# The first two units in thirds of the tokens, and a new order at the start of attention, in a one-core encoder kernel

## The chip, the cores and the metric

One core of one Trainium2 chip runs the whole network. Its engines work side by side and wait for each other on semaphores only: TensorE (PE; PEld is its weight load), VectorE (DVE), ScalarE (ACT), GpSimd (POOL) and SyncE (SP), which here only issues DMAs. The metric is the device time of one execution in microseconds (us), as the median of several runs. In an order of instructions "ps<-xh,wsp" reads: written tile, then read tiles.

## The reference

Two layers over 1040 tokens (16 meta tokens and 1024 real ones) of width 1024, all in f32. Only the beginning matters here:

```python
h = jnp.concatenate([meta, x], axis=1)
hn = rms_norm(h, mix_norm_gain[layer])
z = h @ w_in                                   # w_in: 1024 x 1536
u, q, k, v = jnp.split(z, [D_FOURIER, D_FOURIER + D_ATTN, D_FOURIER + D_ATTN + D_KV], axis=-1)
y_f = fourier_mix(u)                           # a 2-D DFT, real part
q = apply_rope(rms_norm(q...), cos, sin); k = apply_rope(rms_norm(k...), cos, sin)
y_a = attention(q, k, v)                       # 6 query heads, 2 key heads
return jnp.concatenate([y_f, y_a], axis=-1) @ w_out
```

After that come the MLP, a second mixer (hgrn2), a second MLP and a last norm.

## The kernel before

Tokens lie along the free axis, 1044 columns with 4 pads, in three thirds of CB = 348 columns; `h`, `xh` and `xl` are tiles of 8 rows k (the 1024 features over 128 partitions). A product with f32 accuracy is made from two roundings of each operand, a high and a low part: weights `raw` (512 KB, two slots) are split by POOL into `wsp` (L596 high, L598 low), activations by ACT (`xh`, L691) and DVE (`xl`, L1170). A *unit* is one product of all tokens with 128 columns of weights: for each k the three products high*high, high*low, low*high, each over the three thirds, so 72 matmuls of 348 or 344 columns into three banks of PSUM (`ps`), L1799.

**The start.** SP issues, in program order, the small rows, the meta tokens, the eight tiles of x (`xst`, L456), the weights of units 0 and 1 (`raw`, L463), two tables (`dftf`, `sint`), four pieces of the DFT table `tabs` (L481 with 105 partitions, L482 with 101 partitions, for c = 0 and 1), then the weights of unit 2 and on, each of which waits only until the slot has been split. PE turns the nine tiles (L1786, 64 transposes of 128 columns), DVE copies them to `h` (L1166), ACT squares them, then makes `xh` for each k over all tokens, DVE makes `xl`. Units 0 and 1 follow on PE; amid unit 1 stands `first_bcast` (L1845, L1849), which spreads the norm's factors into `rms`, and behind it ACT issues the load of `cost` on its own queue (L732). Then unit 2, the first step of the DFT (L1870), unit 3, the second step (L1888), and units 4 to 11.

POOL splits the weights of unit u when they have landed (`w_land`) and when unit u-1 has begun (`w_used`), so that their slot of `wsp` is free. PE begins unit u when `w_split` says that they are split.

**Attention.** 60 steps; step s scores a tile of 116 queries (L1942, nine matmuls into banks 0 to 2), DVE takes the maximum (three reductions, L1365, then L1367 and L1370), ACT makes the exponentials (L807) and the scaled copy (L819), and PE turns the probabilities (L1969). PE begins the scores of step s when the exponentials of s-1 are made; the transposes of step s-1 need banks 3 to 5, in which the first turned pieces of V lie until DVE has made their low halves `vtl` (L1306, five pieces `v_low(0)` to `v_low(4)`, in banks 3 to 7). `q_join(7)` (L1300) adds the two parts of the last query head, which no step needs before much later.

Of the kernel before, what the change touches and what calls it, by code (L numbers as in the profile page):

```python
# [17 lines left out]
F32 = mybir.dt.float32  # L18
F32R = mybir.dt.float32r
U8 = mybir.dt.uint8  # L20
ALU = mybir.AluOpType
# [3 lines left out]
P = 128  # L25
# [53 lines left out]
def encoder(nc, x, meta, mix_gain, ab_w_in, q_gain, k_gain, ab_w_out, c_w_in, lb_logits, o_gain,  # L79
# [3 lines left out]
    with ctx:  # L83
# [33 lines left out]
        xst = at("xst", [P, 9, 1024], F32, o_x)  # L117
# [114 lines left out]
        v_init = sem("dve_init")  # L232
        n_hi = sem("x_high")
# [126 lines left out]

        def pieces(a):
            return a.rearrange("p (a b) -> p a b", b=CB)
# [84 lines left out]
        def _(sp):  # L447
# [7 lines left out]
            for i in range(1, 9):  # L455
                nc.sync.dma_start(xst[:, i, :], x_rows[(i - 1) * P:i * P, :]).then_inc(s_x[i], 16)  # L456
# [18 lines left out]
            for j, col in enumerate(AB_COLS):  # L475
                load(U_MIX0 + j, j % 2, k8, v_in[:, :, col * P:(col + 1) * P], first=j < 2)
                if j == 1:
                    nc.sync.dma_start(dftf[:], dft_feat).then_inc(s_tab, 16)
                    nc.sync.dma_start(sint[:], sin_tab).then_inc(s_tab, 16)
                    for c in range(2):  # L480
                        nc.sync.dma_start(tabs[0:DN, c, 0:4, :], dft_tok[c, 0:4 * DN].rearrange("(j p) m -> p j m", p=DN)).then_inc(s_tab, 16)  # L481
                        nc.sync.dma_start(tabs[0:HALF + 1 - 4 * DN, c, 4, :], dft_tok[c, 4 * DN:HALF + 1]).then_inc(s_tab, 16)  # L482
# [193 lines left out]
        def _(act):  # L676
# [4 lines left out]
            for i in range(9):  # L681
# [6 lines left out]
            def first_high(k):  # L688
                act.wait_ge(t_dve, 18)
                act.wait_ge(x_sq, 9)  # L690
                A(xh[:, k, :], h[:, k, :], ACT.Copy, scale=small[:, NORM_COL[0] + k:NORM_COL[0] + k + 1]).then_inc(n_hi, 1)  # L691
# [36 lines left out]
            for k in range(KT):  # L728
                first_high(k)
# [414 lines left out]
        def _(dve):  # L1144
# [17 lines left out]
            for i in range(9):  # L1162
                t0, n = in_block(i)
                for half in range(2):
                    dve.wait_ge(t_rdy, 2 * i + half + 1)
                    V.tensor_copy(h[:, 4 * half:4 * half + 4, t0:t0 + n], ps[:, (2 * i + half) % 8, :].rearrange("p (k t) -> p k t", k=4)[:, :, 0:n]).then_inc(t_dve, 1)  # L1166

            def first_low(k):
                dve.wait_ge(n_hi, k + 1)
                V.scalar_tensor_tensor(xl[:, k, :], h[:, k, :], small[:, NORM_COL[0] + k:NORM_COL[0] + k + 1], xh[:, k, :],  # L1170
                                       ALU.mult, ALU.subtract).then_inc(n_lo, 1)
# [39 lines left out]
            dve.wait_ge(t_dve, 18)  # L1211
            clear_pads()
            for k in range(KT):
                first_low(k)
# [136 lines left out]
            def attend(b, s):  # L1351
# [35 lines left out]
            v_low(0)  # L1387
            v_low(1)
            q_scales()
            q_join(7)  # L1390
# [377 lines left out]
        def _(pe):  # L1768
# [6 lines left out]
            for i in range(9):  # L1775
                t0, n = in_block(i)
                pe.wait_ge(s_x[i], 16)
                for half in range(2):
                    g = 2 * i + half
                    if g == 7:  # L1780
                        pe.wait_ge(g_cp, 1)
                    if g >= 8:

                        pe.wait_ge(t_dve, g - 7)
                    for k in range(4):
                        ins = nc.tensor.transpose(ps[:, g % 8, k * P:k * P + n], xst[0:n, i, (4 * half + k) * P:(4 * half + k + 1) * P], ident[0:n, 0:n])  # L1786
                    ins.then_inc(t_rdy, 1)

            pe.wait_ge(t_dve, 18)
# [69 lines left out]
            unit(0, 0, 0, 0, hx, lx, x_ready(0))  # L1859
            unit(1, 1, 1, 1, hx, lx, gap=[first_bcast])  # L1860
# [69 lines left out]
            def attend(b, s):  # L1930
# [411 lines left out]
```

## Time and profile before

| | |
|---|---|
| median of 3 runs | 2677.04 us (2675.21 to 2677.28) |
| the profiled execution, its own time | 2674.69 us |
| its span on the page | 2672.9 us |
| PE busy | 2607.0 us, 98% |
| DVE, ACT, POOL busy | 58%, 34%, 42% |
| mean granted TensorE clock | 0.993 |

The span is what the profiler saw between the first and the last instruction; the execution's own time is 1.79 us more. All times inside the kernel are read from this one execution, counted from the start of the span.

### The profile page before, as it was taken

The page shows a single profiled execution, that of the slowest core. Times are in us where ns is not written, and L with a number is a line of the kernel's source. Part 1 is how long each engine was busy: PE and PEld are TensorE (multiplying, and loading weights), DVE is VectorE, ACT ScalarE, POOL GpSimd, SP SyncE. Part 2 cuts the span into 40 slices and gives each one's busy share as a digit, 9 for nine tenths or more (in the row PEclk, how much of TensorE's full clock was granted, in tenths as well). Part 3 has the DMA queues.
Part 4 walks back from the last instruction along what each step waited for, and adds up shares of the span by engine and source line. Part 5 has one row for each costly group of instructions (what it writes and reads, how often), then busy time and mean ns, then how long its engine had stood idle before and what let it go on. Part 6 is the DMA issues. An engine that isn't in the chain of part 4 may idle for free.

```text
span 2672.9 us, 44728 instructions
## 1 busy us (share of the span) xinstructions
PE 2607.0 (98%) x18627; PEld 2346.5 (88%) x18627; DVE 1553.9 (58%) x1843; ACT 913.3 (34%) x1496; POOL 1125.8 (42%) x599
## 2 busy tenths in 40 slices
PE   7998999999999999999999999999999999999998
PEld 7997998999999999999888888887877888788887
DVE  5398887465545433335676777778485444444444
ACT  3117886133333100013344344434243333210003
POOL 3240001347777444444232232234337878444441
PEclk9999999999999999999999999999999999999999
DMA  5110000122233322222111111112112333422221
GB/s 164 32 40 1 0 0 11 45 80 96 104 113 127 120 96 96 96 86 98 41 33 36 38 33 38 36 33 92 42 49 103 105 117 107 142 99 95 94 88 71
DMA packets 175990, 193.42 MB, mean 72 GB/s; under 512 B 7762, under 2 KB 145316, under 8 KB 175814
## 3 DMA queue, kind: packets, MB, share of 16 engines
q1 hardware_dynamic: 157238, 152.29, 17.4%
q10 hardware_dynamic: 18576, 38.55, 3.8%
q8 instruction: 138, 2.26, 0.4%
q14 instruction: 38, 0.31, 0.0%
HBM read 148.61 MB, written 42.21 MB: 71 GB/s over the span
## 4 chain that ended last, share of the span: by engine, by line
PE 83%; DVE 8%; issue 4%; ACT 3%; DMA 1%; POOL 1%; SPq 0%; ACTq 0%; DVEq 0%; POOLq 0%
PE ps L1799 53%; PE ps L2055 9%; PE ps L2052 5%; PE ps L2053 5%; PE ps L1942 3%; PE ps L2153 2%; PE ps L2121 1%; PE ps L2091 1%; DVE kk L1638 1%; DMA tmp<-hidden 1%; ACT prob L807 1%; PE ps L1888 1%; PE ps L2191 1%; ACT kk L1018 1%; DVE kk L1635 1%
## 5 line engine op out<-in xcount | busy, mean ns | idle before, releaser
L596 POOL TENSOR_TENSOR wsp<-raw,ones 128x1024 fp32r<-128x1024 f32 x140 | 275.2, 1966 | 1340.6 <-PE ps L1799 1303.5
L1799 PE MATMUL ps<-xh,wsp 128*128 128x348 f32 (+2 forms) x2624 | 622.8, 358 | 9.3 <-POOL wsp L598 6.1
L1799 PE MATMUL ps<-hh,wsp 128*128 128x348 f32 (+1 forms) x2480 | 546.2, 350 | 0.0
L1799 PEld LDWEIGHTS ps<-xh,wsp 128*128 128x128 f32 x2624 | 449.5, 189 | 54.9 <-issue 11.5
L1799 PEld LDWEIGHTS ps<-hh,wsp 128*128 128x128 f32 x2480 | 428.8, 188 | 44.1
L598 POOL TENSOR_TENSOR wsp<-raw,wsp 128x1024 fp32r<-128x1024 f32 x140 | 398.0, 2843 | 11.0
L1799 PE MATMUL ps<-xl,wsp 128*128 128x348 f32 (+2 forms) x1312 | 333.9, 351 | 0.0
L1799 PE MATMUL ps<-hl,wsp 128*128 128x348 f32 (+2 forms) x1240 | 313.9, 350 | 0.0
L1799 PEld LDWEIGHTS ps<-xl,wsp 128*128 128x128 f32 x1312 | 232.4, 189 | 24.3
L1799 PEld LDWEIGHTS ps<-hl,wsp 128*128 128x128 f32 x1240 | 218.1, 188 | 22.3
L910 ACT ACTIVATE hh<-tmp 128x1040 fp32r<-128x1040 f32 (+1 forms) x64 | 68.3, 1068 | 491.5 <-DMA tmp<-hidden 369.6
L1411 DVE TENSOR_TENSOR h<-h,ps 128x1024 f32<-128x1024 f32 x80 | 97.5, 1219 | 207.9 <-PE ps L1799 202.3
L1412 DVE TENSOR_TENSOR h<-h,ps 128x1044 f32<-128x1044 f32 x72 | 89.4, 1241 | 219.4 <-PE ps L1799 217.2
L618 POOL TENSOR_TENSOR wop<-sw,wop 128x512 fp32r<-128x512 f32 x112 | 144.3, 1298 | 69.3 <-ACT wop L876 69.2
L618 POOL TENSOR_TENSOR wop<-raw,wop 128x512 fp32r<-128x512 f32 x84 | 132.4, 1576 | 68.1 <-ACT wop L876 68.1
L1460 DVE SCALAR_TENSOR_TENSOR hid<-hid,rms 128x520 f32<-128x520 f32 (+1 forms) x112 | 150.9, 1365 | 0.9
L881 ACT ACTIVATE hid<-hid 128x520 f32<-128x520 f32 (+1 forms) x112 | 71.0, 634 | 229.3 <-DVE hid L1460 229.3
L1466 DVE TENSOR_TENSOR hl<-tmp,hh 128x1040 fp32r<-128x1040 f32 (+1 forms) x64 | 122.3, 1911 | 39.5 <-ACT hh L910 39.5
L1044 ACT ACTIVATE kp<-kk 128x512 f32<-128x512 f32 x112 | 65.6, 635 | 164.0 <-PE ps L2153 145.9
L2055 PE MATMUL ps<-xh,wop 128*128 128x512 f32 x336 | 109.5, 393 | 0.0
L876 ACT ACTIVATE wop<-sw 128x512 fp32r<-128x512 f32 x112 | 70.4, 629 | 113.4 <-PE ps L2053 48.2
L608 POOL TENSOR_TENSOR sw<-sw,raw 128x512 f32<-128x512 f32 x56 | 91.3, 1631 | 2.2
(311 smaller groups left out, 4971.1 us busy)
## 6 DMA issues: line engine op xcount, KB each, us to landing
raw<-in_w SPq DMA_DIRECT2D x128, 512.0 KB, 3.9
raw<-in_c_w_in SPq DMA_DIRECT2D x40, 512.0 KB, 3.8
tmp<-hidden SPq DMA_DIRECT2D x32, 520.0 KB, 4.2
tmp<-hidden SPq DMA_DIRECT2D x32, 512.0 KB, 4.2
hidden<-hid ACTq DMA_DIRECT2D x56, 260.0 KB, 2.1
hidden<-hid ACTq DMA_DIRECT2D x56, 256.0 KB, 2.1
raw<-in_ab_w_in SPq DMA_DIRECT2D x12, 512.0 KB, 3.7
xst<-in_x SPq DMA_DIRECT2D x8, 512.0 KB, 6.5
```

Source lines behind the costliest of these rows:

```text
L596: nc.gpsimd.tensor_tensor(wsp[:, slot, 0, :], raw[:, slot, :], one, ALU.mult).then_inc(w_high, 1)
L598: nc.gpsimd.tensor_tensor(wsp[:, slot, 1, :], raw[:, slot, :], wsp[:, slot, 0, :], ALU.subtract).then_inc(w_split, 1)
L608: nc.gpsimd.tensor_tensor(a[:], left, right, op).then_inc(t_add, 1)
L618: nc.gpsimd.tensor_tensor(operand(g, 1), a, operand(g, 0), ALU.subtract).then_inc(t_low, 1)
L1411: return V.tensor_tensor(real_pieces(h[:, k, :]), real_pieces(h[:, k, :]), real_outp(s), ALU.add).then_inc(z_free, 1)
L1412: return V.tensor_tensor(pieces(h[:, k, :]), pieces(h[:, k, :]), outp(s), ALU.add).then_inc(z_free, 1)
L1460: V.scalar_tensor_tensor(hid_[b][:], hid_[b][:], 0.0, rms[:, span(layer, b % 2)], ALU.max, ALU.mult).then_inc(t_relu, 1)
L1466: V.tensor_tensor(hl[t // CH % 2][:, t % CH, where], tmp[:, t % 2, where], hh[t // CH % 2][:, t % CH, where], ALU.subtract).then_inc(l_l, 1)
L1799: ins = M(ps[:, 3 * s + c, 0:n], w(a, k), b(k)[:, c0:c0 + n], start=(k == first and a == 0 and b is xa), stop=(k == last and a == 1))
L2052: M(out[:, 0, :], left, x(k)[:, 0:width // 2], start=start, stop=stop)
L2053: ins = M(out[:, 1, :], left, x(k)[:, width // 2:width], start=start, stop=stop)
L2055: ins = M(out, left, x(k), start=start, stop=stop)
```

## The change

1. **The order of loads.** The weights of unit 0 are issued ahead of the tiles of x, those of unit 1 behind the third tile. `tabs` comes next, then the weights of unit 2; `dftf` and `sint` stand behind these, with a wait for the last transpose and the last square, since `xst` now lies on their place (it no longer lies on `xh` and `xl`).
2. **Units 0 and 1 by thirds.** ACT and DVE make `xh` and `xl` in pieces of 348 columns, the first third as soon as tiles 0 to 3 are copied. PE makes third(0,0), third(1,0), third(0,1), third(1,1), third(0,2), `first_bcast`, third(1,2), 24 matmuls each (third(u,c): unit u, third c); the transposes of tiles 4 to 8 stand in between, in banks 6 and 7. `w_used` for unit 1 comes with the first matmul of third(1,2).
3. **The start of attention.** `v_low(0)` and `v_low(1)` move from ahead of step 0 to behind its reductions, `q_join(7)` and `v_low(2)` behind its reciprocal, `v_low(3)` and `v_low(4)` into step 1. PE waits for single pieces of `vtl` ahead of the transposes of steps 1 and 2.

```diff
-            for i in range(1, 9):
+            def x_load(i):
                 nc.sync.dma_start(xst[:, i, :], x_rows[(i - 1) * P:i * P, :]).then_inc(s_x[i], 16)
...
+            in_load(0)
+            for i in range(1, 4):
+                x_load(i)
+            in_load(1)
+            for i in range(4, 9):
+                x_load(i)
+            for c in range(2):
+                nc.sync.dma_start(tabs[0:DN, c, 0:4, :], ...).then_inc(s_tab, 16)
+                nc.sync.dma_start(tabs[0:HALF + 1 - 4 * DN, c, 4, :], ...).then_inc(s_tab, 16)
+            in_load(2)
+            sp.wait_ge(t_rdy, 18)
+            sp.wait_ge(x_sq, 9)
+            nc.sync.dma_start(dftf[:], dft_feat).then_inc(s_tab, 16)
+            nc.sync.dma_start(sint[:], sin_tab).then_inc(s_tab, 16)
+            for j in range(3, 12):
+                in_load(j)
...
-            for k in range(KT):
-                first_high(k)
+            for i in range(3):
+                x_square(i)
+            first_high(0)
+            for i in range(3, 6):
+                x_square(i)
+            first_high(1)
+            for i in range(6, 8):
+                x_square(i)
+            first_high(2)
+            x_square(8)
...
-            dve.wait_ge(t_dve, 18)
+            for i in range(4):
+                x_copy(i)
+            dve.wait_ge(t_dve, 8)
             clear_pads()
             for k in range(KT):
-                first_low(k)
+                first_low(0, k)
+                if k in (1, 3, 5):
+                    x_copy(4 + k // 2)
+            x_copy(7)
+            x_copy(8)
+            for c in range(1, 3):
+                for k in range(KT):
+                    first_low(c, k)
             first_norm()
...
                 if not begun(b, s, 1):
-                    dve.wait_ge(r_q, 6)
-                    for g in range(2, 5):
-                        v_low(g)
+                    v_low(0)
+                    v_low(1)
+                elif not begun(b, s, 2):
+                    v_low(3)
+                    v_low(4)
                 if not drained(b, s, 0):
                     dve.wait_ge(a_exp, b * 6 + (s + 1))
                     V.reciprocal(col[6], col[5]).then_inc(a_rc, 1)
+                if not begun(b, s, 1):
+                    q_join(7)
+                    dve.wait_ge(r_q, 6)
+                    v_low(2)
...
-            v_low(0)
-            v_low(1)
             q_scales()
-            q_join(7)
...
-            unit(0, 0, 0, 0, hx, lx, x_ready(0))
-            unit(1, 1, 1, 1, hx, lx, gap=[first_bcast])
+            def third(u, c, turns=()):
+                c0, n = ALL[c]
+                if c == 0:
+                    pe.wait_ge(w_split, u + 1)
+                for k in range(KT):
+                    if u == 0:
+                        pe.wait_ge(n_hi if c == 2 else f_hi, k + 1 if c == 2 else 8 * c + k + 1)
+                        pe.wait_ge(n_lo if c == 2 else f_lo, k + 1 if c == 2 else 8 * c + k + 1)
+                    for a, b in ((0, hx), (0, lx), (1, hx)):
+                        ins = M(ps[:, 3 * u + c, 0:n], wsp[:, u, a, k * P:(k + 1) * P], b(k)[:, c0:c0 + n],
+                                start=(k == 0 and a == 0 and b is hx), stop=(k == KT - 1 and a == 1))
+                        if u == 1 and c == 2 and k == 0 and a == 0 and b is hx:
+                            ins.then_inc(w_used, 1)
+                    if k % 2 and k // 2 < len(turns):
+                        x_turn(turns[k // 2])
+                if c == 2:
+                    ins.then_inc(z_ready, 1)
+
+            third(0, 0, (4, 5, 6))
+            third(1, 0, (7, 8))
+            third(0, 1)
+            third(1, 1)
+            third(0, 2)
+            first_bcast()
+            third(1, 2)
             unit(2, 0, 2, 0, hx, lx)
...
                     pe.wait_ge(a_p, b * 6 + s)
-                    if not begun(b, s, 2):
-                        pe.wait_ge(av_l, 5)
                     for r in range(3):
+                        if not begun(b, s, 3):
+                            pe.wait_ge(av_l, r + 1 if s == 1 else (4, 5, 5)[r])
```

SP's queue before, from the meta tokens to the weights of units 2 and on:

```order
L454 DMA xst<-in_meta 16x1024
L456 DMA xst<-in_x 128x1024 x8
L463 DMA raw<-in_ab_w_in 128x8x128 x2
L478 DMA dftf<-in_dft_feat 128x256
L479 DMA sint<-in_sin_tab 128x1044
L481 DMA tabs<-in_dft_tok 105x4x522
L482 DMA tabs<-in_dft_tok 101x522
L481 DMA tabs<-in_dft_tok 105x4x522
L482 DMA tabs<-in_dft_tok 101x522
L463 DMA raw<-in_ab_w_in 128x8x128 x10
```

And in the changed kernel, up to the weights of unit 3 and on:

```order
L460 DMA xst<-in_meta 16x1024
L470 DMA raw<-in_ab_w_in 128x8x128
L463 DMA xst<-in_x 128x1024 x3
L470 DMA raw<-in_ab_w_in 128x8x128
L463 DMA xst<-in_x 128x1024 x5
L493 DMA tabs<-in_dft_tok 105x4x522
L494 DMA tabs<-in_dft_tok 101x522
L493 DMA tabs<-in_dft_tok 105x4x522
L494 DMA tabs<-in_dft_tok 101x522
L470 DMA raw<-in_ab_w_in 128x8x128
L498 DMA dftf<-in_dft_feat 128x256
L499 DMA sint<-in_sin_tab 128x1044
```

The two small tables have left their place ahead of `tabs`; the four pieces of `tabs` still stand ahead of the weights of unit 2.

DVE's instructions before, from the last query head's factor (`qsc`) to the second step of attention:

```order
L1312 RECIPROCAL qsc<-qsc 116x54
L1313 TENSOR_SCALAR nqsc<-qsc 116x54
L1314 TENSOR_SCALAR qsc<-qsc 116x54
L1300 TENSOR_TENSOR y<-tmp,rot 128x1044
L1365 TENSOR_REDUCE amax<-ps 116x1 x3
L1367 SCALAR_TENSOR_TENSOR amax<-amax,nqsc 116x1
L1370 SCALAR_TENSOR_TENSOR amax<-amax,nqsc 116x1
L1306 TENSOR_TENSOR vtl<-ps,vth 116x512 x2
L1306 TENSOR_TENSOR vtl<-ps,vth 116x256
L1381 RECIPROCAL amax<-amax 116x1
L1365 TENSOR_REDUCE amax<-ps 116x1 x3
```

And the same place in the changed kernel:

```order
L1355 RECIPROCAL qsc<-qsc 116x54
L1356 TENSOR_SCALAR nqsc<-qsc 116x54
L1357 TENSOR_SCALAR qsc<-qsc 116x54
L1408 TENSOR_REDUCE amax<-ps 116x1 x3
L1410 SCALAR_TENSOR_TENSOR amax<-amax,nqsc 116x1
L1413 SCALAR_TENSOR_TENSOR amax<-amax,nqsc 116x1
L1349 TENSOR_TENSOR vtl<-ps,vth 116x512 x2
L1426 RECIPROCAL amax<-amax 116x1
L1343 TENSOR_TENSOR y<-tmp,rot 128x1044
L1349 TENSOR_TENSOR vtl<-ps,vth 116x512
L1408 TENSOR_REDUCE amax<-ps 116x1 x3
```

The reductions of step 0 follow at once on the factors; two `vtl` pieces (which stood ahead of `qsc`) and the join `y<-tmp,rot` now stand behind them, the join and one `vtl` piece ahead of the reductions of step 1.

## Rows read from the trace of the kernel before

**Rows 1.** The page: the span, and the chain that ended last by engine.
```profile
span 2672.9 us, 44728 instructions
...
PE 83%; DVE 8%; issue 4%; ACT 3%; DMA 1%; POOL 1%; SPq 0%; ACTq 0%; DVEq 0%; POOLq 0%
```

**Rows 2.** The chain of waits, 0 to 64 us: start us, us, what.
```profile
31.44 13.08 PE ps L1799 x81
...
46.75 17.11 PE ps L1799 x108
```

**Rows 3.** Waits of PE, 0 to 340 us: total us, times, longest us.
```profile
PE ps L1942 <- ACT prob L807: 6.6, 7, 5.2
PE ps L1799 <- POOL wsp L598: 6.1, 1, 6.1
```

**Rows 4.** POOL in order of time, 0 to 60 us: start us, us, instruction [idle before].
```profile
47.12 1.90 POOL L596 TENSOR_TENSOR wsp<-raw,ones 128x1024 fp32r<-128x1024 f32 x1 [16.93 <-DMA raw<-in_ab_w_in]
49.10 2.39 POOL L598 TENSOR_TENSOR wsp<-raw,wsp 128x1024 fp32r<-128x1024 f32 x1
52.76 1.90 POOL L596 TENSOR_TENSOR wsp<-raw,ones 128x1024 fp32r<-128x1024 f32 x1 [1.27 <-PE ps L1799]
54.73 2.81 POOL L598 TENSOR_TENSOR wsp<-raw,wsp 128x1024 fp32r<-128x1024 f32 x1
```

**Rows 5.** The queue of SP at 26 us: start us, us in issuing, instruction.
```profile
26.90 9.30 SPq L463 DMA_DIRECT2D raw<-in_ab_w_in  x1
```

**Rows 6.** Line 463 in the first 200 us: from issue to landing.
```profile
DMA to landing us min/median/max: 3.5/3.7/20.1
```

**Rows 7.** DMA issues of the first 110 us: KB each, median us to landing.
```profile
sint<-in_sin_tab SPq DMA_DIRECT2D x1, 522.0 KB
cost<-in_cos_tab ACTq DMA_DIRECT2D x1, 522.0 KB, 4.1
tabs<-in_dft_tok SPq DMA_DIRECT2D x2, 205.9 KB
dftf<-in_dft_feat SPq DMA_DIRECT2D x1, 128.0 KB
```

**Rows 8.** Busy time by stretch: at the end PEclk, DMA share, GB/s.
```profile
29.00:37.00 8.00, 6.80 (x43) 6.54 (x42) 7.96 (x8) 0.31 (x2) 1.20 (x1) 1.00 0.09 29
39.00:42.00 3.00, 3.00 (x21) 3.00 (x20) 0.00 (x0) 0.00 (x0) 0.00 (x0) 1.00 0.06 25
```

**Rows 9.** The same view, around two stretches in which PE had stood idle.
```profile
24.05:27.70 3.65, 3.62 (x13) 3.65 (x14) 3.65 (x2) 3.65 (x4) 3.57 (x2) 0.50 0.76 188
...
207.60:212.00 4.40, 0.00 (x0) 0.00 (x0) 4.23 (x11) 1.06 (x2) 0.00 (x0) 1.00 0.00 0
212.00:222.20 10.20, 8.21 (x30) 7.33 (x30) 6.04 (x17) 5.77 (x11) 0.00 (x0) 0.50 0.01 2
```

**Rows 10.** Line 1170 in the first 50 us: ns min/median/max.
```profile
L1170 DVE SCALAR_TENSOR_TENSOR xl<-h,small,xh x8: 1293/1351/3439, 20.3 to 34.9; 128x1044 fp32r<-128x1044 f32 x8
```

**Rows 11.** Line 1166 in the first 50 us: ns min/median/max.
```profile
L1166 DVE COPY h<-ps x18: 224/680/692, 6.6 to 18.4; 128x512 f32<-128x512 f32 x16, 128x64 f32<-128x64 f32 x2
```

**Rows 12.** The chain of waits, 200 to 228 us.
```profile
206.29 1.29 DVE vtl L1306 x2
...
208.33 1.25 DVE y L1300
...
211.35 1.32 ACT prob L807 x2
...
212.71 2.96 PE ps L1942 x9
...
216.71 1.32 ACT prob L807 x2
...
222.06 1.31 ACT prob L807 x2
...
226.22 1.31 ACT prob L807 x2
```

More of the change, by code:

```diff
@@ L114, in encoder @@
         e_c = o_c + 1484 + 72 + 432 + 32
-        xst = at("xst", [P, 9, 1024], F32, o_x)
+        xst = at("xst", [P, 9, 1024], F32, o_d + 5 * row)
         sqx = at("sqx", [P, 1024], F32, o_t + 2 * row)
@@ L359, in encoder, with x_bank @@
         OG, QG, KG, LB = 40, 48, 49, 50
+        def x_bank(g):
+            return g if g < 8 else 6 + g % 2
         def pieces(a):
@@ L474, in _, with in_load @@
             v_in = ab_w_in.rearrange("(k p) n -> p k n", p=P)
[L475 to L482, printed above, removed]
+            def in_load(j):
+                load(U_MIX0 + j, j % 2, k8, v_in[:, :, AB_COLS[j] * P:(AB_COLS[j] + 1) * P], first=j < 2)
+            in_load(0)
[5 more added lines that the diff above has]
+            for c in range(2):
+                nc.sync.dma_start(tabs[0:DN, c, 0:4, :], dft_tok[c, 0:4 * DN].rearrange("(j p) m -> p j m", p=DN)).then_inc(s_tab, 16)
+                nc.sync.dma_start(tabs[0:HALF + 1 - 4 * DN, c, 4, :], dft_tok[c, 4 * DN:HALF + 1]).then_inc(s_tab, 16)
+            in_load(2)
[5 more added lines that the diff above has]
+                in_load(j)
             v_out = ab_w_out.rearrange("(k p) n -> p k n", p=P)
@@ L680, in _, with x_square @@
             act.wait_ge(v_init, 1)
-            for i in range(9):
+            def x_square(i):
                 n = in_block(i)[1]
@@ L686, in _, with first_high @@
                 A(sqx[0:n, :], xst[0:n, i, :], ACT.Square, accum_out=stat[0:n, 0, i:i + 1]).then_inc(x_sq, 1)
[L688 to L691, printed above, removed]
+            def first_high(c):
+                act.wait_ge(t_dve, (8, 14, 18)[c])
+                third = slice(c * CB, (c + 1) * CB)
+                for k in range(KT):
+                    A(xh[:, k, third], h[:, k, third], ACT.Copy, scale=small[:, NORM_COL[0] + k:NORM_COL[0] + k + 1]).then_inc(n_hi if c == 2 else f_hi, 1)
             def first_norm():
@@ L1161, in _, with x_copy @@
             V.tensor_copy(small[:, :], ps[:, 7, 0:SROWS]).then_inc(g_cp, 1)
-            for i in range(9):
+            def x_copy(i):
                 t0, n = in_block(i)
@@ L1165, in _, with first_low @@
                     dve.wait_ge(t_rdy, 2 * i + half + 1)
[L1166 to L1171, printed above, removed]
+                    V.tensor_copy(h[:, 4 * half:4 * half + 4, t0:t0 + n], ps[:, x_bank(2 * i + half), :].rearrange("p (k t) -> p k t", k=4)[:, :, 0:n]).then_inc(t_dve, 1)
+            def first_low(c, k):
+                third = slice(c * CB, (c + 1) * CB)
+                dve.wait_ge(n_hi if c == 2 else f_hi, k + 1 if c == 2 else 8 * c + k + 1)
+                V.scalar_tensor_tensor(xl[:, k, third], h[:, k, third], small[:, NORM_COL[0] + k:NORM_COL[0] + k + 1], xh[:, k, third],
+                                       ALU.mult, ALU.subtract).then_inc(n_lo if c == 2 else f_lo, 1)
             def first_norm():
@@ L1774, in _, with x_turn @@
             nc.tensor.transpose(ps[:, 7, 0:SROWS], srow[0:SROWS, :], ident[0:SROWS, 0:SROWS]).then_inc(g_rdy, 1)
-            for i in range(9):
-                t0, n = in_block(i)
+            def x_turn(i):
+                n = in_block(i)[1]
                 pe.wait_ge(s_x[i], 16)
@@ L1782, in _ @@
                     if g >= 8:
-                        pe.wait_ge(t_dve, g - 7)
+                        pe.wait_ge(t_dve, g - 1)
                     for k in range(4):
-                        ins = nc.tensor.transpose(ps[:, g % 8, k * P:k * P + n], xst[0:n, i, (4 * half + k) * P:(4 * half + k + 1) * P], ident[0:n, 0:n])
+                        ins = nc.tensor.transpose(ps[:, x_bank(g), k * P:k * P + n], xst[0:n, i, (4 * half + k) * P:(4 * half + k + 1) * P], ident[0:n, 0:n])
                     ins.then_inc(t_rdy, 1)
-            pe.wait_ge(t_dve, 18)
+            for i in range(4):
+                x_turn(i)
             def blocks(s, w, xa, xb, ks, first, last, ready=None, opens=True, cols=ALL):
```

4 lines of the change are left out of this document (added).

## The prediction

> **What bounds the kernel now.** The page's chain of waits is 83% PE [rows 1], so each microsecond by which PE's stream ends a stage earlier counts, and one for which PE waits for something else counts too. The change touches two stages, the first 64 us and the first steps of attention, so I read the chain of waits there, then who waited for whom, and then each queue by itself.
>
> In the start PE waited 6.1 us for the first split weights [rows 3], lost a little more to `xl`, and from 31.44 us ran without a gap: 81 matmuls of units 0 and 1, the broadcast, then from 46.75 us 108 matmuls in 17.11 us, which are the second half of unit 1 and all of unit 2 [rows 2]. That is 0.158 us each, so unit 2 began at 46.75 + 36 x 0.158 = 52.4 us and ended at 63.9. **The change can gain in the start only what it brings unit 2 forward.**
>
> So the reader should look at what else unit 2 needs: its weights. POOL began to split them at 47.12 us, after 16.93 us of idling that their DMA ended [rows 4]. The split was done at 49.10 + 2.39 = 51.5 us, only 0.9 us before PE wanted it. Their DMA was issued at 26.90 us, sat 9.30 us in SP's queue [rows 5] and landed 20.1 us after its issue [rows 6], though a usual one takes 3.7 us. Why? From 29 to 37 and from 39 to 42 us the DMA share is 0.09 and 0.06, and 29 and 25 GB/s move [rows 8]: that is one of 16 DMA engines at work. The transfers in front are the pieces of `tabs` with 101 partitions, 205.9 KB each [rows 7]; at 25 GB/s one of them takes 8.4 us, and there are two. One engine works through both, and the share of unit 2's weights that this engine carries stands behind them.
>
> In attention PE waited once 5.2 us for ACT [rows 3]. The chain there runs through DVE: two low halves of V, 1.29 us, the join, 1.25 us, then reductions and the exponentials at 211.35 us [rows 12].
>
> **The start, term by term.** PE's own work stays: 144 matmuls, 64 transposes, one broadcast. The end of unit 1: DVE can copy tile 1 about 1.3 us later than before (512 KB of weights in front at 16 x 25 GB/s), say from 10.5 us. Up to the copies of tile 8 it has 16 copies of 0.68 us [rows 11] = 10.9 and 8 lows of a third, between 1.29/3 = 0.43 and, beside POOL's splits, 3.44/3 = 1.15 us [rows 10], so 3.4 to 9.2 us. That is 25 to 31 us, 28 in the middle. From there PE has four thirds of 24 x 0.158 = 3.8 us and the broadcast, which took 46.75 - 44.52 = 2.2 us (13.08 us from 31.44 end at 44.52) [rows 2]: unit 1 ends at 28 + 17.4 = **45 us** (42 to 48), about 7 us before 52.4. ACT's 24 smaller copies lie beside this.
>
> Unit 2's weights: ahead of them in the loaded engine stand all that stood there, less `dftf` and `sint`, 650 KB [rows 7], 1/16 of it, 41.6 thousand bytes, at 25 GB/s 1.7 us. So they land not at 47.0 but at **45.3 us**. But the broadcast is now over at about 28 + 11.4 + 2.2 = 41.6 us, and behind it ACT issues `cost`, 522 KB [rows 7], whose sixteenth costs an engine 1.3 us. Before, it went out at the end of the broadcast at 46.8 us, too late to matter. Whether two queues share an engine, no row shows; its cost is 0 to 1.3 us. I take 1.3, since in the stretch of rows 8 that engine has not a moment free: landing at 46.6 us. The Trainium skill says the same (DMA: Bandwidth & Descriptors, section "Issuing engines are not separate DMA queues"): transfers of all issuing engines run on the same 16 and interleave. By that page the landing is at 46.6 us, and without it at 45.3; no row here shows which.
>
> Then POOL: 1.90 and 2.39 us and a gap, 4.4 us alone, or 4.8 us with the low half at 2.81 us beside DVE's folding [rows 4]. Unit 1 ending at 45, the folding falls just there, so 4.8. Unit 2 begins at 46.7 + 4.8 + 0.2 = **51.7 us**, against 52.4: 0.7 us gained (2.5 us with both better bounds).
>
> The gap that takes the place: PE, done at 45, idles 6.7 us. What PE's clock does after such a pause stands in rows 9: after an idle 4.40 us the granted clock was 0.50, that is 1.2 GHz of 2.4, for 10.20 us; in the start, after the 6.1 us, it was 0.50 from 24.05 to 27.70 us, in which PE made 13 matmuls, 0.28 us each, though it was never idle. Before, these slow ones cost nothing, as `xl` was later anyway. Now they fall into unit 2. At the 3.65 us of that row PE makes 13 where 23 would fit: **1.6 us lost**; at twice this, 3.2. Sum of the start: +0.7 - 1.6 = **0.9 us lost** (from 2.5 gained to 2.5 lost). Units 3 and on follow as before: with the two small tables now ahead of its weights in the loaded engine, unit 3 has them at some 46.6 + 1.7 + 1.3 = 49.6 us, and POOL waits for unit 2's first matmul. `dftf` and `sint`, landing behind unit 2's weights at some 48 us, are needed at 63.
>
> **Attention, term by term.** Two low halves, 1.29 us, and the join, 1.25 us, leave the chain ahead of step 0. The scores were ready at 207.6 (PE is idle from there [rows 9]), the factors now at 208.33 - 1.29 = 207.0; the third reduction can only start at about 207.9, so of the 2.5 us **2.4 us** are gained, the exponentials beginning at 208.95. The two low halves fall under the exponentials (1.32 us). Join and third low half, 1.9 us, now follow the reciprocal; behind them in DVE's queue wait the reductions of step 1, and for those ACT. Step 1's scores take 2.96 us at the low clock [rows 12] and are ready about 3.0 us after the exponentials' end, so the 1.9 us are covered; at the high clock they end the wait, and the step then lasts as long. The last two low halves, 1.0 us, lie under step 1's exponentials. The edit's worth is 2.4 us if the clock falls as before. If it does not, since PE now idles 2.9 us and not 5.2 [rows 3], one period shrinks from 222.06 - 216.71 = 5.35 to 226.22 - 222.06 = 4.16 us: 3.6 us. I take 2.4: the pause is still long, and PE stands still again for as long in the next step.
>
> **Sum.** -2.4 + 0.9 = 1.5 us less: the profiled execution's own 2674.7 becomes 2673.2, and on the median of the runs shown, 2.3 us above it, 2677.0 becomes **2675.5 us**. What a measurement of this kernel tells from no change is some 0.2%, 5.4 us.
>
> **Rivals.** (a) *Unit 2's weights don't gate it*: the loaded engine is through much sooner, and PE goes on at 45 us. For it: unit 2's weights do stand nearer to the front. Against: the 101-partition pieces stand in front of them in the new order too, 16.8 us of one engine. Worth 7.4 us in the start, 9.8 to 11 in all: 2667. 8%. (b) *The gate stands, but everything else goes well*: `cost` doesn't delay the landing, POOL is alone, the clock recovers in less than 3.65 us, and stays up in attention: 2.5 - 1 + 3.6 = 5.1 us, up to 6: 2671 to 2672. 13%. (c) *Slower: PE makes the thirds at the low clock.* Between tiles it waits for small pieces, and if the granted clock falls then, a third takes 24 x 0.28 = 6.7 us. Six of them from 15 us on, with the broadcast and the transposes, end at about 60 us, and unit 2 begins 7.6 us later than before; less 2.4 that is +5.2: 2682. It decides once unit 1 ends after 51.7 us. For it: 0.50 in rows 9 while PE was busy. Against: a third without waits is 24 matmuls in a row, and the low clock of rows 9 ended after 3.65 us of such work. 6%. (d) *The two edits cancel altogether*, twice the slow stretch and no gain from the landing: 2677 to 2678. This is the likeliest case's other end. The likeliest, with (d), has the remaining 73%, 2673 to 2678.5.
>
> **How the numbers follow.** Faster by over 0.2% is case (a) and the best part of (b): 12%. Slower by over 0.2% needs 5.4 us: half of (c) and what I don't see, 5%. The same: 83%. The range leaves out (a) and (c) and takes in most of (b): 2671.0 to 2679.0.
>
> **What would show it.** In the changed profile POOL should begin its third high half (unit 2) at 46 to 47 us, released by the DMA of `raw`; PE should wait some 5 to 8 us for it, and its clock should then be 0.50 for 3 to 7 us. The first exponentials of attention should begin about 2.4 us nearer to the last matmul of unit 11. The prediction is wrong if POOL has those weights before 40 us, or if unit 1 ends after 51 us.

## The result and the profile after

| | changed kernel | before, beside it |
|---|---|---|
| median | 2681.1 us (2679.2 to 2685.3, 14 runs) | 2676.6 us (2672.9 to 2679.5, 14 runs) |
| ratio | 1.0019, 95% interval 1.0011 to 1.0028 | |
| profiled execution, its own time | 2683.44 us | 2674.69 us |
| its span | 2681.7 us | 2672.9 us |

The kernel has become slower by 4.5 us by the medians, some 0.2%. I had 2675.5 us and a range up to 2679.0. One of the 12 runs of `pad_before`, a kernel of experiment 6, took 6534.6 us and is in neither its median nor its ratio below. The page of the changed kernel, against [rows 1]: the chain's shares have hardly moved, so the page alone doesn't say where the time went.

```profile
span 2681.7 us, 44770 instructions
...
PE 83%; DVE 7%; issue 4%; ACT 3%; DMA 1%; SPq 1%; POOL 1%; ACTq 0%; DVEq 0%; POOLq 0%
```

The chain of waits of the changed kernel in the start (start us, us, what) does, where [rows 2] had PE without a gap from 31.44 us:

```profile
25.98 19.19 DMA raw<-in_ab_w_in
45.20 0.04 POOLq L614
45.24 6.53 issue
51.77 0.04 POOLq L616
51.81 1.90 POOL wsp L615
53.78 2.38 POOL wsp L617
56.16 0.04 issue
56.21 11.68 PE ps L1847 x72
```

The weights of unit 2 landed at 25.98 + 19.19 = 45.2 us, as forecast. But then 6.5 us pass in which nothing is charged: POOL had its data and waited for something else. POOL in order of time, against [rows 4], names it:

```profile
51.80 1.89 POOL L615 TENSOR_TENSOR wsp<-raw,ones 128x1024 fp32r<-128x1024 f32 x1 [33.41 <-PE ps L1917]
53.78 2.38 POOL L617 TENSOR_TENSOR wsp<-raw,wsp 128x1024 fp32r<-128x1024 f32 x1
```

It was released by PE (L1917 is `third`), by `w_used`, the first matmul of third(1,2). Before, the releaser was the DMA. So unit 2 is no longer gated by its weights but by unit 1 itself, and starts at 56.2 us instead of 52.4. Why is unit 1 so late? DVE in order of time (L1198 copies a tile's half, L1204 is a third's `xl`) shows it:

```profile
21.75 0.69 DVE L1198 COPY h<-ps 128x512 f32<-128x512 f32 x1 [2.48 <-PE ps L1833]
22.60 0.69 DVE L1198 COPY h<-ps 128x512 f32<-128x512 f32 x1 [0.16 <-PE ps L1833]
23.21 1.06 DVE L1204 SCALAR_TENSOR_TENSOR xl<-h,small,xh 128x348 fp32r<-128x348 f32 x2
25.61 1.29 DVE L1198 COPY h<-ps 128x512 f32<-128x512 f32 x2 [1.34 <-PE ps L1833]
26.82 1.06 DVE L1204 SCALAR_TENSOR_TENSOR xl<-h,small,xh 128x348 fp32r<-128x348 f32 x2
29.23 1.29 DVE L1198 COPY h<-ps 128x512 f32<-128x512 f32 x2 [1.34 <-PE ps L1833]
30.43 1.06 DVE L1204 SCALAR_TENSOR_TENSOR xl<-h,small,xh 128x348 fp32r<-128x348 f32 x2
33.78 1.29 DVE L1198 COPY h<-ps 128x512 f32<-128x512 f32 x2 [2.29 <-PE ps L1833]
35.61 1.29 DVE L1198 COPY h<-ps 128x512 f32<-128x512 f32 x2 [0.54 <-PE ps L1833]
36.82 7.96 DVE L1204 SCALAR_TENSOR_TENSOR xl<-h,small,xh 128x348 fp32r<-128x348 f32 x16
```

And PE over one round of the same stretch (L1833 are the transposes):

```profile
27.54 0.40 PE L1917 MATMUL ps<-xh,wsp 128*128 128x348 f32 x1 [1.53 <-DVE xl L1204]
27.77 0.32 PE L1917 MATMUL ps<-xl,wsp 128*128 128x348 f32 x1
27.94 0.50 PE L1917 MATMUL ps<-xh,wsp 128*128 128x348 f32 x2
28.27 0.32 PE L1917 MATMUL ps<-xl,wsp 128*128 128x348 f32 x1
28.43 0.32 PE L1917 MATMUL ps<-xh,wsp 128*128 128x348 f32 x1
28.59 1.04 PE L1833 MATMUL ps<-ident,xst 128*128 128x128 f32 x8
```

The two engines work in turn. DVE's next copies wait for the eight transposes of the next tile. In PE's program these stand behind six matmuls, and those wait for the lows that DVE has just made. One round is 3.6 us (25.61 to 29.23), though DVE has only 2.3 us of work in it and PE only 2.1. DVE's five longer idle pieces above add up to 8.0 us, and the copies of tile 8 end at 36.9 us.

In attention the chain against [rows 12] reads:

```profile
211.17 1.37 DVE amax L1408 x3
...
213.03 1.32 ACT prob L838 x2
214.39 2.96 PE ps L2014 x9
...
218.38 1.32 ACT prob L838 x2
```

Everything from the first DFT step up to here stands 4.02 us later than before, so without the second part the exponentials would begin at 215.37; they begin at 213.03: 2.34 us gained.

### The profile page after: what moved, and what is told of

It reads as the page before. It is cut to its first block, busy times and chain, and to the rows that moved or that the text cites. A ratio compares the mean times of both kernels' runs of the same rounds, so it can differ in the third digit from the quotient of the medians.

```text
span 2681.7 us, 44770 instructions
## 1 busy us (share of the span) xinstructions
PE 2612.5 (97%) x18627; PEld 2350.9 (88%) x18627; DVE 1555.7 (58%) x1859; ACT 915.5 (34%) x1512; POOL 1121.9 (42%) x599
## 4 chain that ended last, share of the span: by engine, by line
PE 83%; DVE 7%; issue 4%; ACT 3%; DMA 1%; SPq 1%; POOL 1%; ACTq 0%; DVEq 0%; POOLq 0%
PE ps L1847 52%; PE ps L2127 9%; PE ps L2124 5%; PE ps L2125 5%; PE ps L2014 3%; PE ps L2225 2%; PE ps L2193 1%; PE ps L2163 1%; DVE kk L1684 1%; DMA raw<-in_ab_w_in 1%; ACT prob L838 1%; PE ps L1960 1%; PE ps L2263 1%; ACT kk L1049 1%; DMA tmp<-hidden 1%
## 5 line engine op out<-in xcount | busy, mean ns | idle before, releaser
L1847 PE MATMUL ps<-xh,wsp 128*128 128x512 f32 (+2 forms) x2528 | 603.0, 359 | 2.6 <-DVE xl L1745 1.0
L1847 PEld LDWEIGHTS ps<-xh,wsp 128*128 128x128 f32 x2528 | 432.7, 189 | 48.0 <-issue 2.9
L1847 PE MATMUL ps<-xl,wsp 128*128 128x512 f32 (+2 forms) x1264 | 323.6, 353 | 0.0
L1847 PEld LDWEIGHTS ps<-xl,wsp 128*128 128x128 f32 x1264 | 223.7, 188 | 24.3
L1516 DVE TENSOR_TENSOR hid<-uv,ps 128x520 f32<-128x520 f32 (+1 forms) x84 | 57.4, 685 | 59.9 <-PE ps L2125 30.6
```

The costliest lines, as they stand in the source:

```text
L1847: ins = M(ps[:, 3 * s + c, 0:n], w(a, k), b(k)[:, c0:c0 + n], start=(k == first and a == 0 and b is xa), stop=(k == last and a == 1))
```

## Experiments

The kernels are compared by their medians and by three places of their traces: where the first DFT step begins (S, the end of unit 2), the first exponentials (E), and POOL's first high half behind attention (M).

| kernel | S | E | M | median us | ratio (95%) |
|---|---|---|---|---|---|
| before | 63.87 | 211.35 | 447.03 | 2676.6 | |
| `before_again` | 64.91 | 212.39 | 446.97 | 2675.55 | 1.0003 (0.9994 to 1.0012) |
| `pad_before` | 64.78 | 212.26 | 447.27 | 2677.79 | 1.0007 (0.9998 to 1.0016) |
| changed | 67.89 | 213.03 | 449.15 | 2681.1 | 1.0019 (1.0011 to 1.0028) |
| `after_again` | 69.90 | 216.58 | 453.37 | 2682.94 | 1.0024 (1.0013 to 1.0035) |
| `thirds_only` | 68.96 | 217.97 | 452.88 | 2683.99 | 1.0029 (1.0018 to 1.0040) |
| `tabs_spread` | 69.50 | 214.63 | 452.62 | 2683.57 (one run) | |
| `x_first` | 73.71 | 218.85 | 456.59 | 2686.83 | 1.0043 (1.0028 to 1.0058) |
| `turn_ahead` | 62.21 | 208.91 | 443.89 | 2676.6 | 1.0001 (0.9992 to 1.0010) |
| `ahead_tabs_mid` | 60.89 | 206.03 | 442.81 | 2675.77 | 1.0007 (0.9998 to 1.0016) |
| `order_only` | 65.83 | 212.49 | 447.72 | 2675.59 | 0.9999 (0.9990 to 1.0008) |
| `attn_only` | 64.84 | 209.98 | 445.31 | 2673.70 | 0.9991 (0.9982 to 1.0000) |
| `attn_only_again` | 64.26 | 209.40 | 444.90 | 2673.54 | 0.9991 (0.9982 to 1.0000) |

The kernels ran in three further sittings (occasions of timing, each on another chip), and each ratio is against before in the same sitting. Before came to 2676.1 us for `attn_only`, `thirds_only`, `turn_ahead` and `x_first`, to 2675.5 for `pad_before`, `after_again`, `ahead_tabs_mid` and `tabs_spread`, and to 2675.2 for the rest. S, E and M are read from one execution of each kernel.

**1. The two parts apart.** `attn_only` is the kernel before with part 3 of the change, `thirds_only` the changed kernel without it. The core of that part, against before:

```diff
-            v_low(0)
-            v_low(1)
             q_scales()
-            q_join(7)
...
+                        if not begun(b, s, 3):
+                            pe.wait_ge(av_l, r + 1 if s == 1 else (4, 5, 5)[r])
```

> The kernel before with the third part of the change alone (the new order at the start of attention). My theory: the change's two halves add up, and this one gives back what the profile of the changed kernel shows, 2.35 us at the first exponentials: the first exponentials begin at 209.0 us (before 211.35), the first high half of the weights behind attention at about 444.9 us (before 447.03), and the time is about 2 us below before, a ratio of 0.9992. Rival: the new order of DVE costs in later steps what it saves in the first, or upsets the clock; then the marker behind attention stays at 447.0 and the time is that of before or above.

> The changed kernel with attention's beginning as before, so loads and thirds alone. Theory (the thirds are slower, PE and DVE waiting for each other in turn): unit 2 begins at 56.2 us as in the changed kernel, the first exponentials at 215.4 us (before 211.35), the marker behind attention at 451.1 us, the time 4 us above before from this stage, with what comes later up to 6. Rival (the loss is attention's or comes later): first exponentials at 211 to 212 us.

Measured: attention alone 2673.7 us, 2.4 below before, with an interval that reaches just to 1; thirds alone 2684.0, 7.9 above. For the thirds that is more than the 4 to 6 expected, and their exponentials came at 218.0 us and not at 215.4: PE had a granted clock of 0.50 for 10.2 us in the start of this execution, 3.4 in that of the changed kernel, and once more for 3.4 us at 167.6. The chain of `attn_only` in attention:

```profile
209.98 1.32 ACT prob L807 x2
```

From POOL's fourth high half (53.74 us; 52.76 before) to there it is 156.24 us, before 158.59: 2.35 us gained. At M the two traces of this kernel stand 1.7 and 2.1 us ahead of before's. Another sitting gave the same ratio to four places:

> The attention part alone, unchanged, a second time. If its 2.35 us are real, the median is again 2 to 2.5 us below that of before (ratio 0.9991) and the first high half behind attention about 1.7 us earlier; if the first result was luck of the clock, the ratio is 1.000.

So the attention term stands, and the whole loss comes with the other two parts, the order of loads and the thirds.

**2. Is it the turn-taking?** `turn_ahead` moves each tile's transposes one place forward in PE's program and changes nothing else.

```diff
-            for i in range(4):
+            for i in range(5):
                 x_turn(i)
...
-            third(0, 0, (4, 5, 6))
-            third(1, 0, (7, 8))
+            third(0, 0, (5, 6, 7))
+            third(1, 0, (8,))
```

> The changed kernel with the transposes of tiles 4 to 8 each one place earlier on PE: tile 4 ahead of third(0,0), tiles 5, 6, 7 behind its k = 1, 3, 5, tile 8 behind k = 1 of third(1,0). DVE's order stays. Theory (in the changed kernel DVE waits for a transpose which stands behind matmuls that wait for DVE, five rounds of 3.6 us one after the other): a round shrinks to what DVE does, 2 lows and 2 copies, 2.35 us; the copies of tile 8 end at 30 to 31 us (changed kernel 36.9), unit 1 at 49 to 50 (55.3), unit 2 begins at 50 to 51 (56.2; before 52.4), the marker behind attention lies at 443 to 444 us (changed 449.15, before 447.03), the time is 5 to 6 us below the changed kernel's. Rival 1 (DVE itself is too slow): rounds stay at 3.6 us, nothing changes. Rival 2 (DMA landings of x pace it): the same, nothing changes.

DVE in order of time in `turn_ahead`:

```profile
19.21 1.27 DVE L1198 COPY h<-ps 128x512 f32<-128x512 f32 x2
20.41 1.06 DVE L1204 SCALAR_TENSOR_TENSOR xl<-h,small,xh 128x348 fp32r<-128x348 f32 x2
21.91 1.29 DVE L1198 COPY h<-ps 128x512 f32<-128x512 f32 x2 [0.44 <-PE ps L1833]
23.12 1.06 DVE L1204 SCALAR_TENSOR_TENSOR xl<-h,small,xh 128x348 fp32r<-128x348 f32 x2
24.10 1.28 DVE L1198 COPY h<-ps 128x512 f32<-128x512 f32 x2
25.30 1.06 DVE L1204 SCALAR_TENSOR_TENSOR xl<-h,small,xh 128x348 fp32r<-128x348 f32 x2
26.28 1.28 DVE L1198 COPY h<-ps 128x512 f32<-128x512 f32 x2
28.65 1.29 DVE L1198 COPY h<-ps 128x512 f32<-128x512 f32 x2 [1.09 <-PE ps L1833]
```

A round is now 2.2 us, DVE's own work; DVE idles 1.5 us instead of 8.0; the copies of tile 8 end at 29.9 us, 7.0 earlier; unit 2 begins at 50.5, 5.7 earlier, and the median is 4.5 us below the changed kernel's, back at that of before. This is the cause of the loss in the start, shown. POOL's split of unit 2, in the same trace:

```profile
46.13 1.90 POOL L615 TENSOR_TENSOR wsp<-raw,ones 128x1024 fp32r<-128x1024 f32 x1 [27.70 <-DMA raw<-in_ab_w_in]
```

Now POOL is released by the DMA, and PE waits 1.2 us for the split. With unit 1 earlier, the weights of unit 2 are the gate after all, as the prediction had it; in the changed kernel the late copies hid that.

**3. Are the tiles of x late because of the weights ahead of them?** `x_first` issues all tiles of x ahead of the weights.

```diff
-            in_load(0)
-            for i in range(1, 4):
-                x_load(i)
-            in_load(1)
-            for i in range(4, 9):
+            for i in range(1, 9):
                 x_load(i)
+            in_load(0)
+            in_load(1)
```

> The changed kernel with all eight tiles of x issued ahead of the weights of units 0 and 1, as before the change. If the order of the loads were what makes the changed kernel slower (it delays the first tile of x from 7.8 to 9.7 us), this would be faster by up to 2 us. By my theory it is slower: the weights of unit 0 land at 18.8 us, are split at 23.1, and since the transposes of tiles 4 to 8 stand behind matmuls that need them, the whole chain of rounds starts about 4 us later: copies of tile 8 end at 40 to 41 us, unit 2 begins at 60, 4 us above the changed kernel.

It is the slowest, 2686.8. The tiles come earlier and the first four are copied by 13.4 us, but PE then waits 11.1 us for the first split weights, and the rounds begin only at 26.3 us. The copies of tile 8 end at 42.7 and unit 2 begins at 62.0, later than the 40 to 41 and 60 expected: the granted clock was 0.50 from 14.2 to 31.3 us. For the thirds the order of loads in the change is better than this one.

**4. Do the weights of unit 2 gate anything?** `tabs_spread` is the changed kernel with the pieces of 101 partitions issued as 96 and 5.

```diff
-                nc.sync.dma_start(tabs[0:HALF + 1 - 4 * DN, c, 4, :], dft_tok[c, 4 * DN:HALF + 1]).then_inc(s_tab, 16)
+                nc.sync.dma_start(tabs[0:96, c, 4, :], dft_tok[c, 4 * DN:4 * DN + 96]).then_inc(s_tab, 16)
+                nc.sync.dma_start(tabs[96:HALF + 1 - 4 * DN, c, 4, :], dft_tok[c, 4 * DN + 96:HALF + 1]).then_inc(s_tab, 16)
```

> The changed kernel with only the 101-partition pieces of tabs issued as 96 and 5 partitions. Prediction's reading: their one loaded DMA engine holds unit 2's weights back; split so, they land by about 30 us instead of 45.2. Theory (the copies of tile 8 are late, and the weights gate nothing): POOL begins unit 2's split at 51.8 us as in the changed kernel and nothing moves. Rival (the weights gate): the split begins several us earlier.

In its chain of waits the weights of unit 2 appear as

```profile
18.74 15.45 DMA raw<-in_ab_w_in
```

They are issued at 18.7 us and land at 34.2, 11 us earlier than in the changed kernel (I had said 30), and POOL still begins at 53.4, released by PE. This bears out the prediction's reading of the one loaded DMA engine, and in the changed kernel it is worth nothing.

`ahead_tabs_mid` joins this with the earlier transposes and brings `w_used` forward by moving the broadcast:

```diff
                     if k % 2 and k // 2 < len(turns):
                         x_turn(turns[k // 2])
+                    if u == 1 and c == 2 and k == 3:
+                        first_bcast()
...
             third(0, 2)
-            first_bcast()
             third(1, 2)
```

> The changed kernel with (1) the transposes of tiles 4 to 8 one place earlier in PE's order, (2) the 101-partition pieces of tabs issued as 96 and 5 partitions, (3) the broadcast amid third(1,2), so that w_used for unit 1 comes some 2 us earlier. Theory: the copies of tile 8 end at about 30 us, the weights of unit 2 land by about 30 us and no longer gate, POOL splits them when third(1,2) has begun, at about 43.5 us, and unit 2 begins at 48 to 49 us, against 52.4 in the kernel before and 56.2 in the changed one: behind attention 5 to 6 us earlier than in the kernel before, so a median of 2671 to 2674, depending on the down stage. Rival, the weights still land at 45 (the small 5-partition pieces and the splitting don't matter): unit 2 at 50.5, as with the earlier transposes alone.

POOL splits from 43.28 us, released by PE, and unit 2 begins at 49.2 us, 3.2 ahead of before, with no wait of PE for POOL; that is 1.3 us ahead of `turn_ahead`, where the weights gated it. At M the kernel is 4.2 us ahead of before. The median is 2675.8, 0.3 above before's and not the 2671 to 2674 expected: the 4.2 us are not in it. The runs fall into 2672.5 to 2675.8 (six) and 2678.9 to 2681.5 (five). The mean granted clock is 0.9930 in the six and 0.9908 in the five, and 0.0022 of 2676 us is 5.9 us, about the distance between the two groups (2674.4 and 2680.1 on average). So something later takes them back in many executions, and it goes with a lower clock.

**5. Only the order of loads.** `order_only` is `attn_only` with whole units, the weights of unit 0 behind the third tile, those of unit 1 behind the sixth, and the pieces of `tabs` split as above. `dftf` and `sint` stand behind `tabs` here too, but ahead of the weights of unit 2. The part that orders the tiles and the weights:

```diff
+            for i in range(1, 4):
+                x_load(i)
+            in_load(0)
+            for i in range(4, 7):
+                x_load(i)
+            in_load(1)
+            for i in range(7, 9):
+                x_load(i)
```

> The attention part and, of the first part, only the order of loads: the weights of unit 0 behind the third tile of x, those of unit 1 behind the sixth, the 101-partition pieces of tabs as 96 and 5 partitions. Units 0 and 1 stay whole, so that PE and DVE never wait for each other in turn. Theory: POOL splits unit 0 at 11 to 16 us and unit 1 by 22 us, the copies of tile 8 end at 20 to 21 us (18.4 before), the lows take 1.35 us each instead of up to 3.4 and end at about 33 us (36.2 before), PE starts unit 0 at 23 us and unit 2 at 49 to 51 us (52.4 before, 56.2 in the changed kernel), so that with attention it is 4 to 6 us ahead at the first high half behind attention and the median is about 2671 to 2673, the best of all. Rival: the copies wait for tiles that land 2.6 us later and the low clock falls into unit 0, unit 2 begins at 52.4 or later, and the kernel equals the attention part alone, 2673.7.

A miss. DVE and PE in order of time, two views:

```profile
22.92 0.69 DVE L1177 COPY h<-ps 128x512 f32<-128x512 f32 x1 [1.32 <-PE ps L1800]
...
25.70 9.82 DVE L1181 SCALAR_TENSOR_TENSOR xl<-h,small,xh 128x1044 fp32r<-128x1044 f32 x8 [1.08 <-ACT xh L702]
```

```profile
19.61 1.09 PE L1800 MATMUL ps<-ident,xst 128*128 128x128 f32 x8 [1.78 <-DMA xst<-in_x]
```

The lows do take 9.82 us in place of 15.8 now that POOL is through, against [rows 10]. But PE waits 6.3 us in all for the tiles, up to 1.8 at a time (1.4 us in all in `attn_only`), with the two loads of weights in between, and the copies end at 24.5 us instead of 19.1. The clock was low for 10.2 us from 21.3 us on, and unit 2 begins at about 54.2 us; both are as the rival had it. One gain pays for the other loss: unit 2 ends 1.0 to 1.6 us later than in `attn_only`, and the median is 2.1 us higher (2675.6 against 2673.5).

**6. What happens behind attention.** From M on the changed kernel keeps its 2.1 us until the down stage of layer 0's MLP, where it loses 5.6 more (POOL's third high half there at 894.63 us, 886.88 before). ACT's high halves there, in the changed kernel (the gap in brackets is the wait for the reload of `tmp` from the buffer `hidden`), then DVE's lows and POOL's splits:

```profile
867.77 1.07 ACT L941 ACTIVATE hh<-tmp 128x1040 fp32r<-128x1040 f32 x1 [2.46 <-DMA tmp<-hidden]
871.75 1.08 ACT L941 ACTIVATE hh<-tmp 128x1040 fp32r<-128x1040 f32 x1 [2.91 <-DMA tmp<-hidden]
```

```profile
872.86 5.86 DVE L1512 TENSOR_TENSOR hl<-tmp,hh 128x1040 fp32r<-128x1040 f32 x2 [1.53 <-ACT hh L941]
```

```profile
872.41 1.89 POOL L669 TENSOR_TENSOR wsp<-raw,ones 128x1024 fp32r<-128x1024 f32 x1 [6.69 <-PE ps L2125]
875.29 2.34 POOL L672 TENSOR_TENSOR wsp<-raw,wsp 128x1024 fp32r<-128x1024 f32 x1 [0.98 <-PE ps L2125]
```

Of two reloads issued together the second comes some 1.5 us late, DVE's two lows then fall beside POOL's splits and take 5.86 us together in place of 1.24 each, and PE starts 2.9 us late (4.9 us of waiting in place of 2.0). PE's next 72 matmuls then take 14.35 us in place of 11.61, since the granted clock is 0.50 for 6.8 us (third number from the end of the row; the view is explained below):

```profile
879.20:886.00 6.80, 5.96 (x21) 6.00 (x22) 3.63 (x4) 1.07 (x1) 4.27 (x2) 0.50 0.40 149
```

2.9 and 2.7 make up the 5.6 us. I ran the changed kernel again, and the kernel before with as many instructions more as the changed one has, to see whether this belongs to the program.

> The changed kernel unchanged, for a second trace of it. Start and attention as in the first: unit 2's split at about 51.8 us, the first exponentials at about 213, the first high half behind attention at about 449. If the loss in the down stage belongs to the program, the first splits of that stage stand again about 8.4 and 13.8 us apart (before: 5.6 and 11.0) and the median is 2681; if to chance, this trace may show 5.6 and 11.0.

> The kernel before with 16 more memsets on DVE and 16 more tiny copies on ACT in the first 7 us, where both engines wait for x anyway: as many instructions more as the changed kernel has. Theory 'layout': the third reload of hidden in the down stage of layer 0 (about 868 us) stands late because of where the instruction fetches fall, and these move with the number of instructions: then the first eight lows of that stage collide with POOL's splits as in the changed kernel (two lows 5.8 us instead of 1.24 each), and the median rises by 2 to 4 us, to about 2679. Rival 'chance': it differs from execution to execution whatever the program: median 2676 to 2677, as before. Up to 800 us the two traces should agree within 0.5 us.

> The kernel before, unchanged, timed as if it were a variant: what the measurement makes of no change, and a second trace of it. Theory 'chance': its mean granted clock can come out at 0.992 as well as at 0.993, as that of the padded kernel did, and its ratio lies within 0.9995 and 1.0007. Rival 'the padding itself costs': median within 0.5 us of the other runs of before and a mean clock of 0.993. The down stage's first splits are 5.6 and 11.0 us apart as in the first trace, or 5.6 and 12.6 with one more clock fall of 3.4 us.

The edit of `pad_before`, against before:

```diff
-            V.memset(ones[:], 1.0).then_inc(v_init, 1)
+            for j in range(16):
+                V.memset(ones[:, 8 * j:8 * j + 8], 1.0).then_inc(v_init, 1)
-            V.memset(h[:, :, TOK:T], 0.0)
+            V.memset(h[:, 0:4, TOK:T], 0.0)
+            V.memset(h[:, 4:8, TOK:T], 0.0)
...
+            for j in range(16):
+                A(sqx[0:1, 8 * j:8 * j + 8], ones[0:1, 0:8], ACT.Copy).then_inc(pad_act, 1)
```

The same place in `after_again`, DVE in order of time:

```profile
875.78 1.24 DVE L1512 TENSOR_TENSOR hl<-tmp,hh 128x1040 fp32r<-128x1040 f32 x1 [0.47 <-ACT hh L941]
878.60 1.27 DVE L1512 TENSOR_TENSOR hl<-tmp,hh 128x1040 fp32r<-128x1040 f32 x1 [1.57 <-ACT hh L941]
```

No collision, in the same program. It stood in three of the seven traces that have thirds (changed, `thirds_only`, `turn_ahead`) and in none of the six with whole units. That is too few to say that the thirds bring it about; it isn't fixed to the program.

The other thing that differs from execution to execution is the clock. Busy time by stretch in the start (stretch, its length, busy us of PE, PEld, DVE, ACT and POOL, then PEclk, DMA share, GB/s), changed kernel and then `after_again`:

```profile
18.80:22.20 3.40, 3.28 (x14) 3.21 (x14) 0.92 (x2) 3.22 (x7) 0.00 (x0) 0.54 0.99 294
22.20:36.90 14.70, 10.29 (x71) 9.37 (x70) 9.03 (x17) 7.17 (x14) 0.00 (x0) 0.99 0.39 112
```

```profile
18.30:28.50 10.20, 7.57 (x28) 6.70 (x28) 4.63 (x8) 4.92 (x10) 0.44 (x1) 0.50 0.81 232
28.50:40.00 11.50, 8.92 (x62) 8.62 (x63) 7.32 (x14) 7.15 (x15) 0.00 (x0) 1.00 0.22 69
```

After nearly the same wait for the first pieces (3.9 and 4.1 us) PE had 1.2 GHz for 3.4 us in one execution and for 10.2 us in the other (10.2 also in `thirds_only` and `tabs_spread`), and S moved from 67.9 to 69.9. In the down stage before's own second trace shows 0.72 from 874 to 878 us where its first has 1.00. Over all runs the mean granted clock was 0.9930, 0.9931 and 0.9934 in before's three sittings, 0.9920 and 0.9918 in the changed kernel's two. A mean clock lower by 0.0012 is 3 us at 2676 us. But `pad_before`, with whole units, also has 0.9918, 11 runs, and is 2.3 us above before by the medians, with an interval that reaches just below 1. Its median, 2677.8, lies between the two forecasts; its trace has no collision, so the theory of the layout falls. That its clock was chance isn't borne out either: `before_again` came out at 2675.6 and 0.9931, as that rival had it. Whether the padding brings the clock down, and by what, is open.

## Why the prediction was wrong, point by point

**The step that failed** is "Up to the copies of tile 8 it has 16 copies ... and 8 lows of a third ... 25 to 31 us, 28 in the middle." The work was right: copies at 0.6 to 0.7 us, and eight lows that took 2.82 + 3 x 1.06 = 6.0 us, inside the 3.4 to 9.2 that I gave (the first two, beside POOL's split, took 1.4 each, above the 1.15 that I had as the most). But I added up one engine's work as if it never waited. It waited 8.0 us in five places, and the copies ended at 36.9; in `turn_ahead`, where it waited 1.5 us, they ended at 29.9, inside the 25 to 31. I had the transposes in PE's program between pairs of k, and did not ask what stood ahead of them there. Adding 17.4 us of thirds and broadcast as the prediction does gives 54.3 us for the end of unit 1; third(1,2) ended at about 55.3. That is past the 51 us that I had named as a sign of being wrong and the 51.7 us that rival (c) named as the point of decision. The number of (c), 2682, came out, but that is mostly luck, since its mechanism is at most a part: the clock was low for 3.4 of the 18 us up to the end of the copies in the profiled execution (10.2 in `after_again`, `thirds_only` and `tabs_spread`), and `turn_ahead`, with 3.4 us of low clock too, is 5.7 us faster by the order alone. The Trainium skill has the rule that I left out (PSUM — Partial Sum Buffer, section "Engine vs sequencer instructions"): matmuls start and complete in program order, and VectorE's queue is strictly first in, first out. The trace agrees: the transposes of 28.59 us, whose banks DVE had copied out by 26.9 us, stood behind a wait of 1.5 us for `xl` and the six matmuls that followed it.

**The landing of unit 2's weights**, 45.3 us without `cost`: 45.2. The `cost` term never came to its test: the broadcast was so late that `cost` was issued at 51.6 us. In `turn_ahead` it went out at 45.6 and the weights landed at 46.0, which tells nothing either. Whether the two would interleave stays open, and so does the rule weighed against it.

**What gates unit 2**: I had the weights landing at 46.6 us, 5 us behind `w_used` at the end of the broadcast, 41.6. In the changed kernel `w_used` came 6.5 us behind the weights. This follows from the late copies: in `turn_ahead` the weights came last.

**The split**, 4.8 us: 1.89 + 2.38 and the gaps, 4.4. The low half took about what it takes alone in [rows 4], 2.39 us, not the 2.81 us that I had put in.

**The clock's 1.6 us in unit 2**: did not occur. PE idled only 0.9 us ahead of it and its clock stayed at 1.00. So unit 2, forecast to begin at 51.7 and to lose 1.6 us inside, began at 56.2 and lost nothing inside: the start lost 4.0 us in place of 0.9 (4.5 over the traces: mean S of the changed kernel's two, `thirds_only` and `tabs_spread` 69.1, of the five with the start of before 64.5).

**Attention**, 2.4 us: 2.34 in the changed kernel, 2.35 alone. The clock fell again for 10.2 us in the changed kernel, as in [rows 9], and for 3.4 us in `attn_only`.

**The rest of the median.** Start and attention give +2.2 us by the means above. That alone would have made 2678.8 us, still inside the range although the mechanism failed. The medians say 4.5 in the first sitting and 7.5 in that of `after_again`. The other 2 to 5 us lie mostly behind M, where the instructions are the same in all kernels. From M to the end of the span the seven traces with thirds take 2227.7 to 2232.5 us, 2229.6 on average, and the five with whole units and no padding 2225.2 to 2227.6, on average 2226.1. The two groups don't overlap, so the 3.5 us between them are not one execution's chance. The collision is at most a part of them: the four traces with thirds that lack it still take 2228.8 on average. Nor is the lower mean clock a term to be added, since the low stretches of the start, of attention and behind the collision are in it. I had left nothing for what lies behind M, and by this the median left the range. Why it is longer there is open; the padded kernel, with whole units, takes 2229.7 too.

**A version that beats both** is `attn_only`: 1.7 to 2.4 us below before in two sittings, each with an interval that reaches just to 1.

## What to carry to other kernels

When two in-order engines feed each other in small pieces, write down for each piece what stands ahead of it in the other's program. If the producer of the next piece stands behind the consumer of the last one, a round costs much more than the larger of the two: here 3.6 us for 2.3 us of work on one engine and 2.1 on the other, and issuing one piece ahead brought it to 2.2 us. And when a gate is named (weights landing at 45.2), check which of the conditions behind the same wait comes last in the new order. For effects of 0.1%, compare a place in the traces as well as the medians: 4.2 us gained at one place were not to be seen in the end.

## What the runs showed that I had not expected

- With two DMAs of 101 partitions ahead of them the next weights were issued at 26.0 us and landed at 45.2; with these issued as 96 + 5 partitions, they were issued at 18.7 and landed at 34.2.
- The same program had its PE clock at 1.2 GHz for 3.4 us in one execution and for 10.2 in another, after nearly the same wait; the start came out 2.0 us apart.
- 32 tiny instructions in idle time at the start came with a mean granted clock of 0.9918 over 11 runs against 0.9931 over 27.
- Behind M, in code that no edit touches, all seven traces with thirds took longer than all five with whole units and no padding, by 3.5 us on average.
- Two DVE subtractions of 1.24 us each took 5.86 us beside POOL's splits. Three of 13 traces had it.
